# Gates of one token block scattered into cleared DRAM by GpSimd, where one-hot products made them

## The reference, cut to what matters

```python
q = (hc @ wq).reshape(t, PEER_HEADS, 2, D_KEY_HALF)
s = jnp.einsum("thpk,pnk->thpn", q, sk)
s1, i1 = lax.top_k(s[:, :, 0], PEER_TOPK)
s2, i2 = lax.top_k(s[:, :, 1], PEER_TOPK)
best, j = lax.top_k(all_sums(s1, s2), PEER_TOPK)      # 16 of 256
e = i1[j // 16] * N_KEYS + i2[j % 16]                 # expert, 0 to 16383
gate = jax.nn.softmax(best, axis=-1)
act = gelu(jnp.einsum("thkd,td->thk", u_tab[e], hc))
out = jnp.einsum("thk,thkd->td", gate * act, v_tab[e])
```

## Time and profile before

| | us |
|---|---|
| median of 3 runs | 2868.94 (2868.77 to 2870.86) |
| the profiled execution, its own time | 2871.31 |
| its span, first to last instruction | 2868.6 |
| TensorE busy in it | 2821.1 (98%) |
| VectorE / ScalarE / GpSimd busy | 2323.8 / 1212.8 / 1189.3 |
| mean granted TensorE clock | 0.996 of full speed |

### The profile page before, as it was taken

The page is one execution under the profiler, slowest core; times in us unless marked ns, Lnnn a source line. Parts: engine busy times, 40 slices in busy tenths (PEclk is TensorE's granted clock), DMA queues, the critical chain, the costliest instruction groups (busy, mean ns, idle before and its releaser), DMA issues.

```text
span 2868.6 us, 46637 instructions
## 1 busy us (share of the span) xinstructions
PE 2821.1 (98%) x15014; PEld 2493.9 (87%) x15014; DVE 2323.8 (81%) x4531; ACT 1212.8 (42%) x1602; POOL 1189.3 (41%) x790
## 2 busy tenths in 40 slices
PE   7999999999999999999999999999999999999998
PEld 5767999999999888888878789999999988888886
DVE  6995799989994888888864608999899758888887
ACT  3443443346663333333332424333566533333333
POOL 2623488872235222222134345888622442222221
PEclk8999999999999999999999999999999999999999
DMA  6436588899998999999844234988999989999995
GB/s 266 143 141 257 199 276 287 291 330 349 366 374 317 347 341 350 343 348 344 319 170 171 78 104 156 316 287 292 324 377 370 354 319 342 350 344 343 348 343 206
DMA packets 301610, 830.70 MB, mean 290 GB/s; under 512 B 29856, under 2 KB 134432, under 8 KB 300832
## 3 DMA queue, kind: packets, MB, share of 16 engines
q1 hardware_dynamic: 180368, 469.57, 46.5%
q0 software_dynamic: 73728, 268.47, 26.2%
q10 hardware_dynamic: 47376, 90.88, 8.3%
HBM read 731.80 MB, written 96.99 MB: 289 GB/s over the span
## 4 chain that ended last, share of the span: by engine, by line
PE 91%; DVE 6%; ACT 1%; issue 1%; DMA 1%; ACTq 1%; POOL 0%; SPq 0%; DVEq 0%
PE bank L1626 12%; PE bank L1677 12%; PE bank L1679 12%; PE bank L1678 12%; PE bank L1628 12%; PE bank L1627 12%; PE bank L1499 4%; PE bank L1501 4%; PE bank L1500 4%; PE bank L1647 3%; DVE rows L1357 2%; PE bank L1604 1%; DVE shared L945 1%; DMA shared<-mod_rows 1%; ACT shared L756 0%
## 5 line engine op out<-in xcount | busy, mean ns | idle before, releaser
L622 ACT ACTIVATE w_hi<-w_raw 128x1024 fp32r<-128x1024 f32 x342 | 361.8, 1059 | 666.4 <-PE bank L1679 655.4
L1677 PE MATMUL bank<-w_hi,h_hi 128*128 128x512 f32 x1536 | 598.3, 390 | 0.0
L1679 PE MATMUL bank<-w_lo,h_hi 128*128 128x512 f32 x1536 | 598.2, 389 | 0.0
L1678 PE MATMUL bank<-w_hi,h_lo 128*128 128x512 f32 x1536 | 598.1, 389 | 0.0
L1626 PE MATMUL bank<-h_hi,w_hi 128*128 128x384 f32 x1376 | 466.0, 339 | 0.0
L1628 PE MATMUL bank<-h_lo,w_hi 128*128 128x384 f32 x1376 | 460.6, 335 | 0.0
L1627 PE MATMUL bank<-h_hi,w_lo 128*128 128x384 f32 x1376 | 460.3, 335 | 0.0
L1227 DVE TENSOR_TENSOR w_lo<-w_raw,w_hi 128x1024 fp32r<-128x1024 f32 x256 | 314.0, 1226 | 178.7 <-ACT w_hi L622 174.1
L1677 PEld LDWEIGHTS bank<-w_hi,h_hi 128*128 128x128 f32 x1536 | 288.5, 188 | 60.1 <-issue 0.5
L1679 PEld LDWEIGHTS bank<-w_lo,h_hi 128*128 128x128 f32 x1536 | 288.5, 188 | 59.7
L1678 PEld LDWEIGHTS bank<-w_hi,h_lo 128*128 128x128 f32 x1536 | 288.5, 188 | 59.6
(11 more groups left out here) (237 smaller groups left out, 5341.2 us busy)
## 6 DMA issues: line engine op xcount, KB each, us to landing
w_raw<-stream SPq DMA_DIRECT2D x600, 512.0 KB
act_dram<-act_words ACTq DMA_DIRECT2D x248, 192.0 KB
act_words<-act_dram SPq DMA_DIRECT2D x248, 192.0 KB, 5.0
gate_dram<-shared ACTq DMA_DIRECT2D x80, 512.0 KB, 5.2
shared<-gate_dram SPq DMA_DIRECT2D x64, 640.0 KB
oh_words<-mod_rows SPq DMA_DIRECT2D x60, 512.0 KB, 4.6
oh_ic<-mod_rows SPq DMA_DIRECT2D x20, 512.0 KB, 5.3
shared<-mod_rows SPq DMA_DIRECT2D x16, 512.0 KB, 14.9
```

What stands on the lines that cost most here:

```text
L622: nc.scalar.activation(hi_of(grp, s), w_raw[:, s, :], ACT.Copy).then_inc(S["hi_ready"], 1)
L1677: MM(o, p_hi, hi, start=start, stop=False)
L1678: MM(o, p_lo, hi, start=False, stop=False)
L1679: ins = MM(o, p_hi, lo, start=False, stop=stop)
```

## The change

Of the three dense blocks, block 1 (128 tokens, `SCATTERED`) no longer passes the rounds. Its two halves of `gate_dram` are cleared first: `clear_gates`, on ScalarE's queue, writes 2 x 4 MB of zeros by two DMAs, in layer 0 ahead of the last evacuation of `ev_in`, in layer 1 between the copy of `c_row` and the first evacuation of `od_in`. VectorE turns block 1's keys into addresses (`sc_idx`) and keeps its gates (`sc_gate`). GpSimd then adds each slot's 128 gates into `gate_dram` by an indirect DMA with an add (`scatter`, 128 of them per layer, 128 x 4 bytes each): one per two tiles from tile 35 to 67, two per tile from 68 to 123. Ahead of scatters 16, 32, ... 112 GpSimd waits until all before have landed, since two heads of a token may pick the same expert. SyncE waits for all of them before it loads the gates.

The rounds shrink to 32 groups, tiles 68 to 99; two of the three transpositions per layer stay. VectorE's low parts reach from tile 72 to 123 and GpSimd's last ones are 124 to 127. The dots that were made behind the rounds are spread over tiles 101 to 123 at 4 per 3 tiles.

```diff
-GROUPS = DT // GROUP
+SCATTERED = P
+SCATTERED_HALVES = SCATTERED // HALF
+BLOCKS = DB - 1
+GROUPED = DT - SCATTERED
+GROUPS = GROUPED // GROUP
-GROUP_LOWS = range(GROUP_TILE + 4, GROUP_TILE + 1 + GROUPS)
+GROUP_LOWS = range(GROUP_TILE + 4, EXPERT_TILES - 4)
+def scatters_to(j):
+    early = max(0, (min(j, GROUP_TILE) - 33) // 2)
+    amid = 2 * max(0, j - GROUP_TILE + 1)
+    return min(SLOTS, early + amid)
...
                 sp.wait_ge(S["g_head"], 16 * (l + 1) * HALVES_OF[1])
+                sp.wait_ge(S["scattered"], 16 * SLOTS * (l + 1))
                 load_gates(tail, 0)
...
+            def scatter(l, n):
+                if n == 0:
+                    pool.wait_ge(S["sc_ready"], l + 1)
+                    pool.wait_ge(S["zeroed"], 16 * SCATTERED_HALVES * (l + 1))
+                if n and n % TOPK == 0:
+                    pool.wait_ge(S["scattered"], 16 * (l * SLOTS + n))
+                nc.gpsimd.indirect_dma_start(
+                    out=gate_words, out_offset=bass.IndirectOffsetOnAxis(ap=sc_idx[:, n:n + 1], axis=0),
+                    in_=sc_gate[:, n:n + 1], in_offset=None, compute_op=ALU.add).then_inc(S["scattered"], 16)
...
                         fetch_u(l, n)
                         n += 1
+                    for m in range(scatters_to(j - 1), scatters_to(j)):
+                        scatter(l, m)
...
+            def clear_gates():
+                for n in range(SCATTERED_HALVES):
+                    act.dma_start(gate_dram[n], zeros[:].unsqueeze(1).to_broadcast([P, NK // QUAD, QUAD * HALF])
+                                  ).then_inc(S["zeroed"], 16)
...
+            act.wait_ge(S["consts"], 1)
+            clear_gates()
             step(EV_IN - 1, u_c[:, AC - 1, :], ACT.Gelu)
...
             nc.scalar.copy(rows[:], c_row[:]).then_inc(S["c_rows"], 1)
+            clear_gates()
             for c in range(KC):
...
+                    if b == 1:
+                        chained(V.tensor_scalar(i_f[:], i_f[:], float(NK * HALF), None, ALU.mult))
+                        chained(V.scalar_tensor_tensor(out=i_f[:], in0=j_f[:], scalar=float(HALF), in1=i_f[:],
+                                                       op0=ALU.mult, op1=ALU.add))
+                        V.tensor_scalar(sc_idx[:], i_f[:], sc_token[:, 0:1], None, ALU.add)
+                        ins = V.tensor_tensor(sc_gate[:].rearrange("p (h k) -> p h k", h=HEADS), gate[:],
+                                              gate_z.unsqueeze(2).to_broadcast([P, HEADS, TOPK]), ALU.mult)
+                        ins.then_inc(S["sc_ready"], 1)
+                        stop_for_dots(b, 5)
+                        return
...
-                for n in range(dots_to(GROUPS), SLOTS):
+                n = dots_to(GROUPS)
+                for j in range(GROUP_TILE + 1 + GROUPS, GROUP_LOWS.stop):
+                    dve.wait_ge(S["hi_ready"], u_first + j + 1)
+                    V.tensor_tensor(u_lo(j), w_raw[:, j % RING, :], u_hi(j).bitcast(F32), ALU.subtract
+                                    ).then_inc(S["lo_ready"], 1)
+                    end = dots_to(GROUPS) + (j - GROUP_TILE - GROUPS) * 4 // 3
+                    while n < min(end, SLOTS):
+                        dot(n)
+                        n += 1
+                while n < SLOTS:
                     dot(n)
+                    n += 1
```

More of the change, by code:

```diff
@@ L96 @@
 QUAD = 4
[L97 removed]
+HALVES_OF = (BLOCKS, BLOCKS - 1)
 STOPS = ((0, 3, 3, 3, 3, 2), (3, 3, 2, 3, 3, 2), (3, 3, 2, 3, 3, 3))
@@ L116 @@
 assert len(FETCH_AFTER) == EARLY + BESIDE + U_RING
-GROUP_LOWS = range(GROUP_TILE + 4, GROUP_TILE + 1 + GROUPS)
-TURN_AFTER = {16 * (b + 1) - 2: b for b in range(1, TB)}
+GROUP_LOWS = range(GROUP_TILE + 4, EXPERT_TILES - 4)
[3 more added lines that the diff above has]
+    return min(SLOTS, early + amid)
+assert scatters_to(EXPERT_TILES - 5) == SLOTS
+TURN_AFTER = {16 * (b + 1) - 2: b for b in range(2, TB)}
 EXP_AHEAD = {6: 0, 22: 1, 40: 2, 57: 3}
@@ L183, in build @@
         v_idx = sb("v_idx", [P, SLOTS], I32)
+        sc_idx = sb("sc_idx", [P, SLOTS], I32)
+        sc_gate = sb("sc_gate", [P, SLOTS])
+        sc_token = sb("sc_token", [P, 2])
+        zeros = sb("zeros", [P, QUAD * HALF])
         dots = sb("dots", [P, SLOTS])
@@ L355, in u_lo @@
             return w_lo_first[:] if j % 3 == 2 else w_lo[:, j % 3, :]
+        gate_words = gate_dram.rearrange("b p o (t u) -> (b p o t) u", u=1)
         stream_rows = stream.rearrange("a p d -> (a p) d")
@@ L476, in _ @@
             nc.gpsimd.iota(iota_i[:], [[1, P]], base=0, channel_multiplier=0)
+            nc.gpsimd.iota(sc_idx[:, 0:1], [[1, 1]], base=0, channel_multiplier=1)
+            nc.gpsimd.memset(zeros[:], 0.0)
             nc.gpsimd.memset(ident[:], 0.0).then_inc(S["pool_chain"], 1)
@@ L737, in store_gates @@
                     act.wait_ge(S["g_ev"], l * 2 * GROUPS + n * 16 + 16 + 2)
-                    act.dma_start(gate_dram[n][:, piece * keys // QUAD:(piece + 1) * keys // QUAD, :],
+                    act.dma_start(gate_dram[SCATTERED_HALVES + n][:, piece * keys // QUAD:(piece + 1) * keys // QUAD, :],
                                   gate_st[:, half, piece * keys:(piece + 1) * keys, :]
@@ L742, in peer_act @@
                 pieces = [range(0, 2), range(2, 4), range(4, 5), range(5, 6), range(6, 7), range(7, 8), (), ()]
-                for n in range(2 * DB):
+                for n in range(2 * BLOCKS):
                     half = n % 2
@@ L1305, in _ @@
             V.tensor_copy(iota_2[:], iota_i[:].unsqueeze(2).to_broadcast([P, P, 2]))
+            link(V.tensor_copy(sc_token[:, 0:1], sc_idx[:, 0:1]))
+            link(V.tensor_scalar(sc_token[:, 1:2], sc_token[:, 0:1], float(HALF), float(P * NK * HALF - HALF),
+                                 ALU.is_ge, ALU.mult))
+            link(V.tensor_tensor(sc_token[:, 0:1], sc_token[:, 0:1], sc_token[:, 1:2], ALU.add))
             V.tensor_copy(iota_r[:], iota_i[:, 0:NCAND].unsqueeze(2).to_broadcast([P, NCAND, HALF_K]))
```

18 lines of the change are left out of this document (9 added, 9 removed).

## The result

The changed kernel takes 3106.26 us (median of 4 runs, 3103.85 to 3108.66) against 2868.86 us: a ratio of 1.0826, 95% interval 1.0812 to 1.0839. It is slower by 237 us. I had forecast slower, but by 35 us (2904 us, range 2842 to 2958), and the measured time lies 148 us above the range.

The account below looks back on a forecast made before the run. TensorE, busy 2821.1 of 2868.6 us, was taken as the bound. The profiled 2871.3 us plus 11 (GpSimd's lateness beyond the groups saved) plus 24 (clearing) gave 2906, less 2.4 against the median 2904 us; range 2842 to 2958.

Parts of the forecast that it names:

- The bound, and what the change takes away: TensorE bounds the kernel; 16 groups fewer per layer save 16.0 us, VectorE's moved work costs nothing.
- What a scatter costs GpSimd ... I take 1.35 us: Each scatter's time on GpSimd, sized from fetches: 1.35 us, between 0.95 and 1.9.
- the upper end, 1.9: Highest time assumed for one scatter on GpSimd: 1.58 us of a disturbed fetch plus a 0.30 gap.
- scatters are dear: Rival: an add in DRAM has no row; at 1.6 us per scatter the kernel takes 2955 us; chance 0.13.
- What a landing costs ... 5.5 us: Ahead of 7 scatters per layer GpSimd waits until all before have landed, 5.5 us each.
- (c): Tiles 72 to 123: GpSimd full, 258 us of work for 245; TensorE waits 9.4 us at tile 124.
- (a) to (c): Three places where GpSimd comes too late: 21.4 us per layer against 16.0 won, so 11 us lost in all.
- (a): Tiles 60 to 71: scatters delay GpSimd's low parts and TensorE waits about 8 us per layer.
- (b): The fetches of tiles 60 to 71 come late and delay VectorE's dots and one-hots: 4 us per layer.
- What the clearing costs: Issuing the clearing holds ScalarE 20.1 us per layer, costing 7.7 us in layer 0, 16.5 in layer 1, together 24.

Follow-up runs that it names:

- no_scatter: The changed kernel without its 256 scatters, keeping the clearing, the 32 groups and VectorE's moved low parts and dots: 2846.73 us, 0.9928 of the kernel before.
- late_scatters: The changed kernel with no scatter ahead of tile 68, all 128 per layer spread evenly over tiles 68 to 123: 3089.52 us.

## Why the prediction was wrong

*The bound, and what the change takes away: right.* From tile 0 to tile 127 layer 0's gelus take 577.2 us before and 559.4 without scatters, layer 1's 578.4 and 564.8: 17.8 and 13.6 us for the 16.0 forecast. VectorE's moved low parts and dots cost nothing, as put.

*"What a scatter costs GpSimd ... I take 1.35 us": the step that failed.* It was sized from fetches. A plain scatter is indeed much like one (0.98 us at the median, 1.07 in the mean, 1.37 with the gap). The add has no row in the trace of before, and it holds GpSimd 0.61 us longer. Issued undisturbed a scatter's pitch is 1.85 us, and in the mean with the gap 2.0. Even the upper end, 1.9, was below that mean. This step is worth 153 us of the loss, by the run with plain writes. The prediction named this as the place where it would fail, and its rival "scatters are dear" names the mechanism that was found; but it was priced at 1.6 us, 2955 us in all, with 0.13, when nothing in the trace excluded more.

*"What a landing costs ... 5.5 us": right as a size* (56.9 / 12 = 4.7 us of waiting; up to 11.8 in a busy stretch). But six of the seven per layer stood in the 258 us of (c), for which nothing was charged; in the kernel's two layers they are 57 us of GpSimd's time.

*(a) to (c), 21.4 us per layer: the second step that failed, beyond the pitch.* With plain writes, whose pitch is the one that I had assumed, the scatters lose 106 us, 53 per layer. I had treated three places and called GpSimd "full" between them, at 258 us of work for 245, and charged nothing for the 13 us that didn't fit. What is left over at each place is handed on. In layer 0 of the changed kernel, against no_scatter, the gelu of tile 60 was 17 us late already, where nothing was forecast although 13 scatters stand ahead of it; tile 72 was 36 us late ((a) and (b) make 12), tile 99 was 70, and tile 124 lost 41 us more beyond tile 123.

*No term for TensorE's clock: missing.* Behind waits stand products at the lower clock: 55.4 us of the 259.5, in TensorE's account. Whether they cost the kernel that much isn't shown: while GpSimd sets the pace, a slower product can pass in time that TensorE would have waited, and the table above gives the loss without a term for them.

*"What the clearing costs", 24 us: wrong in the size of the hold.* It was 11.1 us (0.64 and 10.41) and 8.4 us, for 20.1 in each layer. The way from the hold to the price was sound: the same sums with these holds give nothing in layer 0, where none is to be seen, and 4.8 us in layer 1, where the profiles show 5.2 and the times no difference. The error made the forecast slower and so nearer, by luck: with these holds I would have said 2885. Of the 35 us by which I had forecast a slower kernel, 24 were the clearing's, which was not the cause.

## What to carry to other kernels

Before work is given to a queue, write down the free time of that queue stretch by stretch, gaps between its instructions included, and compare it with all that is added. Below it an operation can be free, if each stretch has room for what stands there (282 us of scatters cost 57 us or nothing by their places); above it this kernel paid microsecond for microsecond. An operation with no row in the trace needs a wide price: here its nearest relative, the fetch, bounded it from below only. A wait for a landing is best put behind other work of the same queue: with pauses ahead of the waits, and the last scatter three tiles earlier, 128 adds cost nothing where they had cost 52 us.

## What the runs showed of the hardware

- An indirect DMA of 128 pieces of 4 bytes takes GpSimd 0.98 us as a plain write and 1.59 us as an add into DRAM (medians); half of the pieces save 0.14 us of the add. It is 32 packets as a plain write and 144 as an add. In GpSimd's rows a low part behind a scatter starts ahead of that scatter's end, and its row then reads 2.96 us for 2.40, so the pitch is the number to use. The Trainium skill says so ("Perfetto Trace Analysis", GPSIMD Engine Instruction): time such instructions from start to start. The rows agree.
- Some of VectorE's instructions take longer beside GpSimd's. Two groups of 11 additions on 128x128 elements, the earlier and the later one, in VectorE's timeline of no_scatter and then of the changed kernel:

```profile
470.47 1.68 DVE L1111 TENSOR_TENSOR oh_words<-oh_words 128x128 f32<-128x128 f32 x11
538.73 3.89 DVE L1111 TENSOR_TENSOR oh_words<-oh_words 128x128 f32<-128x128 f32 x11
...
471.05 5.12 DVE L1116 TENSOR_TENSOR oh_words<-oh_words 128x128 f32<-128x128 f32 x11
547.51 10.39 DVE L1116 TENSOR_TENSOR oh_words<-oh_words 128x128 f32<-128x128 f32 x11
```

  It takes no scatter for that. In late_scatters, which has none there, the earlier group takes 3.83 us, beside a low part of GpSimd's; at 1.68 us GpSimd had no instruction running for most of the group. What the scatters do is fill GpSimd's gaps, so that the low parts meet more of VectorE's work. VectorE is busy for 2277 us in no_scatter and for 2309 in the changed kernel; in late_scatters, with none ahead of tile 68, it is 2281. The Trainium skill gives a mechanism ("SBUF — State Buffer", SBUF: two separate sides): a VectorE operation with two inputs in SBUF and a GpSimd operation that reads SBUF take one port pair in turn, each for a whole instruction. The rows fit it; no run here took it apart.
- A hole of 2.7 us ahead of TensorE delayed the gelus behind it by 5.8 us; the granted clock was 0.70 to 0.73 in the 12 us around it, and 1.00 before and after.
